# A two-model transformer kernel on one core: tiny attention placed between the blocks of the keys' projection, up and output projections as three products of rounded halves, and constant products in three of TensorE's waits

## What is computed

```python
h = modulate(rms_norm(x, norm_mix_g), sh_mix, sc_mix)
p_in = h @ w_in + b_in          # u, v, tq, tk, tv, nq, nk, nv, gates
tiny = tiny_attention(tq, tk, tv, tk_c, tv_c) @ tiny_w_o      # width 64, 256 queries, 512 keys
o_a = spatial_gating(u, v, tiny, ...)                         # 256 x 1024
o_b = neighbourhood_attention(nq, nk, nv, ...)                # 256 x 512
merged = gate_a * (o_a @ w_up_a) + gate_b * (o_b @ w_up_b)    # 1024x1024, 512x1024
x = x + g_mix * (merged @ w_out)                              # 1024x1024
h2 = modulate(rms_norm(x, norm_ffn_g), sh_ffn, sc_ffn)
y = moe_ffn(h2, ...)            # router, shared expert, 64 experts of width 256
```

## Time and profile before

| | us |
|---|---|
| median of three runs | 1713.54 (1712.35 to 1714.54) |
| the profiled execution, its own time | 1710.19 |
| its span, first to last instruction | 1708.3 |
| TensorE busy in it | 1632.5 (96%) |
| mean granted TensorE clock | 0.984 |

### The profile page before, as it was taken

The page is one execution under the profiler, slowest core; times in us unless marked ns, Lnnn a source line. Parts: engine busy times, 40 slices in busy tenths (PEclk is TensorE's granted clock), DMA queues, the critical chain, the costliest instruction groups (busy, mean ns, idle before and its releaser), DMA issues.

```text
span 1708.3 us, 21333 instructions
## 1 busy us (share of the span) xinstructions
PE 1632.5 (96%) x8924; PEld 1118.9 (65%) x8925; DVE 791.3 (46%) x1157; ACT 563.0 (33%) x796; POOL 40.9 (2%) x49
## 2 busy tenths in 40 slices
PE   5999999989999999999997999999999999999998
PEld 2745544447444444445454877799998877799997
DVE  3117934133222222222225685765445685776454
ACT  2013430012111111111113575644433566734341
POOL 0410010000000000000000000000000000000000
PEclk9998999998999999999998999999999999999999
DMA  9944873642999999999993433556546444546450
GB/s 357 283 145 142 307 288 117 251 169 105 390 420 421 421 421 421 420 422 421 421 408 137 170 139 136 197 166 205 168 154 221 149 148 148 197 148 217 155 172 25
DMA packets 148287, 418.52 MB, mean 245 GB/s; under 512 B 6960, under 2 KB 55104, under 8 KB 123168
## 3 DMA queue, kind: packets, MB, share of 16 engines
q1 hardware_dynamic: 134688, 335.15, 53.0%
q10 hardware_dynamic: 8784, 63.97, 9.0%
q0 software_dynamic: 4720, 18.03, 3.5%
HBM read 416.07 MB, written 2.95 MB: 245 GB/s over the span
## 4 chain that ended last, share of the span: by engine, by line
PE 89%; DVE 5%; ACT 2%; issue 1%; SPq 1%; DMA 1%; DVEq 0%; ACTq 0%
PE bank L1303 14%; PE bank L1198 13%; PE bank L1517 12%; PE bank L897 10%; PE bank L1209 7%; PE bank L1467 6%; PE bank L1180 4%; PE bank L1219 3%; PE bank L866 3%; PE bank L1036 3%; PE bank L1488 3%; PE bank L1316 3%; PE bank L910 2%; SPq L704 1%; DVE ring_low L2266 1%
## 5 line engine op out<-in xcount | busy, mean ns | idle before, releaser
L2266 DVE TENSOR_TENSOR ring_low<-weight_ring,high_ring 128x2048 fp32r<-128x2048 f32 x92 | 207.9, 2288 | 58.4 <-ACT high_ring L1669 58.0
L1198 PE MATMUL bank<-weight_ring,arena 128*64 128x512 f32 x800 | 232.4, 593 | 1.7 <-issue 1.0
L1303 PE MATMUL bank<-high_ring,split 128*128 128x512 f32 x608 | 199.7, 402 | 0.8 <-DVE split L2273 0.8
L1669 ACT ACTIVATE high_ring<-weight_ring 128x2048 fp32r<-128x2048 f32 x92 | 171.6, 1905 | 10.5 <-PE bank L1303 5.9
L1198 PEld LDWEIGHTS bank<-weight_ring,arena 128*64 128x64 f32 x800 | 75.4, 137 | 149.1 <-issue 148.9
L897 PE MATMUL bank<-weight_ring,arena 128*128 128x512 f32 (+1 forms) x416 | 165.8, 560 | 3.9 <-ACT arena L1556 3.1
L1517 PE MATMUL bank<-split,ring_low 128*128 128x256 f32 x576 | 162.6, 282 | 0.0
L1303 PE MATMUL bank<-ring_low,split 128*128 128x512 f32 x384 | 154.3, 402 | 0.0
L1517 PE MATMUL bank<-split,high_ring 128*128 128x256 f32 x832 | 148.9, 280 | 0.0
L1303 PEld LDWEIGHTS bank<-high_ring,split 128*128 128x128 f32 x608 | 116.4, 192 | 32.5 <-issue 3.4
L897 PEld LDWEIGHTS bank<-weight_ring,arena 128*128 128x128 f32 x416 | 79.5, 196 | 86.7 <-issue 82.6
(11 more groups left out here) (295 smaller groups left out, 2440.5 us busy)
## 6 DMA issues: line engine op xcount, KB each, us to landing
weight_ring<-in_w_in SPq DMA_DIRECT2D x62, 1024.0 KB, 7.6
weight_ring<-in_w_e_gate SPq DMA_DIRECT2D x49, 1024.0 KB, 9.3
weight_ring<-in_w_e_up SPq DMA_DIRECT2D x49, 1024.0 KB, 12.8
weight_ring<-in_w_e_down ACTq DMA_DIRECT2D x46, 1024.0 KB, 10.0
weight_ring<-in_w_ada SPq DMA_DIRECT2D x24, 1024.0 KB, 13.6
weight_ring<-in_w_ffn_gate SPq DMA_DIRECT2D x22, 1024.0 KB, 5.5
weight_ring<-in_w_ffn_up SPq DMA_DIRECT2D x22, 1024.0 KB, 8.0
weight_ring<-in_w_ffn_down SPq DMA_DIRECT2D x22, 1024.0 KB, 5.3
```

The lines of the kernel that those rows point to most:

```text
L1198: last = mm(hidden_bank[side * CAP:(side + 1) * CAP, :].rearrange("p (j n) -> p j n", n=FF), xgT[:, p // 2 % 2, kt, at:at + CAP], hidden_u ...
L1303: last = mm(bank(key)[:, :], left[:, a_, n, t * P:(t + 1) * P], wv[b_][:, j, :], start=(n == 0 and i == 0), stop=(n == kts * len(units_) - ...
L1669: A(upper(key, layer), ring[:, units.place[key][0], :], ACT.Copy).then_inc(sem("high_ready"), 1)
L2266: V.tensor_tensor(lower(key), ring[:, units.place[key][0], :], upper(key, layer), ALU.subtract)\
```

## The change

On TensorE and with it on the engines that feed it:

- The four steps of the tiny attention (`tiny_turns`, `tiny_scores`, `tiny_probs_turn`, `tiny_sum`) each follow one of the four `nk` blocks; the same steps on ScalarE and VectorE stand between their work on those blocks, and `nv` comes last. `pr` and `prT` lie elsewhere.
- The weights of `upa`, `upb` and `wo` (10 pieces of 128x2048, `FIRST_SPLIT`), the gated rows, `obT` and the merged rows are split into halves; `token_split` takes the place of `token_major`. The gating and the up projections are reordered: the turns of tile 0 stand ahead of the last gating product, and `upa` and `upb` go by column half first, then by tile.
- `keep_busy(key, n)` issues n float32 products of constants into a free bank: 3 ahead of the `tiny` projections, 4 ahead of the turns of `h2`, 7 ahead of the second model's first turns, and 1 more in each of its two layers ahead of `vs`. Their results are not used.
- Loads: only the first of the shared expert's three is issued ahead of the last piece of `wo`; the other two follow the first six expert pieces and wait for the last two `wo` groups. The router's weights are loaded at the end of the gated rows' turns, the final norm's row later.

```diff
+FIRST_SPLIT = [("upa", 0, 0), ("upa", 0, 1), ("upb", 0), ("upa", 1, 0), ("upa", 1, 1), ("upb", 1),
+               ("wo", 0, 0), ("wo", 0, 1), ("wo", 1, 0), ("wo", 1, 1)]
+FIRST_UPPER = [20480, 24576, 10240, 22528, 12288, 24576, 20480, 10240, 22528, 12288]
...
-        oaT, mT = area(6144, KT, S), area(8192, KT, S)
+        oas = split[:, 6144:10240].rearrange("p (w k t) -> p w k t", w=2, k=KT)
+        obs = routed[:, 5888:7936].rearrange("p (w f t) -> p w f t", w=2, f=4)
         xn, cn = area(10240, TT, D), area(12288, TT, D)
...
+                        else:
+                            wait_full(sp, ("wo", 0, 1))
                     elif j == 0:
...
+            for j in (1, 2):
+                wait_full(sp, ("wo", j - 1, 1))
+                load_shared(j)
...
 
             wait_out(pool, ("oaT", 3))
-            pool.dma_start(fin_g, bcast("final_norm_g", 0, D)).then_inc(sem("fin_landed"), 16)
-            wait_full(pool, ("upb", 1, 1))
             pool.dma_start(w_rt, a["w_router"].rearrange("(k p) n -> p k n", p=P)).then_inc(sem("router_landed"), 16)
             pool.dma_start(rt_b, bcast("b_router", 0, E)).then_inc(sem("router_landed"), 16)
+            wait_full(pool, ("upb", 1, 1))
+            pool.dma_start(fin_g, bcast("final_norm_g", 0, D)).then_inc(sem("fin_landed"), 16)
...
+            def token_split(key, left, t, units_, kts, it, between=None):
+                wait_bank(pe, key, it)
+                n = 0
+                for uk in units_:
+                    if n and between:
+                        between()
+                    wait_split(pe, uk, it)
+                    wv = halves(uk, CHUNK, it)
+                    for j in range(kts):
+                        for i, (a_, b_) in enumerate(PASSES):
+                            last = mm(bank(key)[:, :], left[:, a_, n, t * P:(t + 1) * P], wv[b_][:, j, :],
+                                      start=(n == 0 and i == 0), stop=(n == kts * len(units_) - 1 and i == 2))
+                        n += 1
+                full(last, key)
...
+            def keep_busy(key, n, it=0):
+                wait_bank(pe, key, it)
+                for _ in range(n):
+                    mm(bank(key)[:, :], k("ident"), const[:, 0:CHUNK], start=True, stop=True)
...
+            keep_busy(("tiny", 0), 3)
...
-            for f in range(4):
+            def tiny_turns():
+                pe.wait_ge(sem("tiny_roped"), 1)
+                turns(("tqT", 0), [tqkv[:, t, 0:TINY] for t in range(TT)])
+                turns(("tkT", 0), [tqkv[:, t, TINY:2 * TINY] for t in range(4)])
+            def tiny_scores():
+                wait_out(pe, ("tqT", 0))
...
+            def tiny_probs_turn():
+                for t in range(TT):
...
+            def tiny_sum():
+                for t in range(TT):
+                    wait_out(pe, ("tpT", t))
+                    wait_bank(pe, ("tO", t))
...
+            for f, tiny_step in enumerate((tiny_turns, tiny_scores, tiny_probs_turn, tiny_sum)):
                 feature_major(("nk", f), hT.rearrange("p w k t -> p k w t"), 2 * S, both(("win", "nk")), (f,))
+                tiny_step()
...
+            gating(0, 0)
+            gating(0, 1)
+            gating(1, 0)
+            gated_turn(0)
+            gating(1, 1)
+            wait_tile(("oaT",), 0)
+            token_split(("upa", 0, 0), oas, 0, both(("upa", 0)), 4, 0)
+            gated_turn(1)
+            pe.wait_ge(sem("ob_low"), 1)
+            token_split(("upb", 0, 0), obs, 0, [("upb", 0)], 4, 0)
+            wait_tile(("oaT",), 1)
+            token_split(("upa", 0, 1), oas, 1, both(("upa", 0)), 4, 0)
+            token_split(("upb", 0, 1), obs, 1, [("upb", 0)], 4, 0)
+            token_split(("upa", 1, 0), oas, 0, both(("upa", 1)), 4, 0)
+            token_split(("upb", 1, 0), obs, 0, [("upb", 1)], 4, 0)
+            token_split(("upa", 1, 1), oas, 1, both(("upa", 1)), 4, 0)
+            pe.wait_ge(sem("merged"), 3)
             turn_tile(("mT",), mg, 0)
+            token_split(("upb", 1, 1), obs, 1, [("upb", 1)], 4, 0)
             wait_tile(("mT",), 0)
-            token_major(("wo", 0, 0), mT, 0, both(("wo", 0)), 4)
-            pe.wait_ge(sem("merged"), 2 * TT)
+            token_split(("wo", 0, 0), oas, 0, both(("wo", 0)), 4, 0)
+            pe.wait_ge(sem("merged"), 4)
             turn_tile(("mT",), mg, 1)
-            token_major(("wo", 1, 0), mT, 0, both(("wo", 1)), 4)
+            token_split(("wo", 1, 0), oas, 0, both(("wo", 1)), 4, 0)
             wait_tile(("mT",), 1)
             for n in range(2):
-                token_major(("wo", n, 1), mT, 1, both(("wo", n)), 4)
+                token_split(("wo", n, 1), oas, 1, both(("wo", n)), 4, 0)
+            keep_busy(("h2T", 0), 4)
             for t in range(TT):
...
+                if layer == 0:
+                    keep_busy(("l_xT", 0), 7)
                 input_turn(0)
+                keep_busy(("vs", 0), 1, layer)
                 wait_out(pe, ("l_xT", 0), layer)
...
+            def first_high(*key):
+                wait_weights(act, key)
+                A(upper(key, 0), ring[:, units.place[key][0], :], ACT.Copy).then_inc(sem("first_high_ready"), 1)
+            def first_turned(name, t):
+                for half in range(2):
+                    wait_full(act, (name, 2 * t + half))
+                    A(oas[:, 0, 4 * half:4 * half + 4, t * P:(t + 1) * P],
+                      bank((name, 2 * t + half))[:, :].rearrange("p (a b) -> p a b", b=P), ACT.Copy)\
+                        .then_inc(sem("first_turned"), 1)
...
+                    first_high("upa", 0, 0)
...
+            first_high("upa", 0, 1)
+            wait_full(act, ("row", 7))
+            wait_out(act, ("nrm", 1))
+            A(obs[:, 0], obT, ACT.Copy).then_inc(sem("ob_high"), 1)
+            first_turned("oaT", 0)
+            wait_full(act, ("sg", 1, 1))
+            first_high("upb", 0)
+            first_high("upa", 1, 0)
+            first_turned("oaT", 1)
+            first_high("upa", 1, 1)
...
+            first_high("upb", 1)
+            first_high("wo", 0, 0)
+            wait_full(act, ("upb", 0, 1))
+            first_high("wo", 0, 1)
+            first_turned("mT", 0)
+            wait_full(act, ("upa", 1, 1))
+            first_high("wo", 1, 0)
+            first_high("wo", 1, 1)
+            first_turned("mT", 1)
...
+            keys_low(0)
             dve.wait_ge(sem("nq_high"), 1)
             V.tensor_tensor(nqs[:, 1], nq32, nqs[:, 0], ALU.subtract).then_inc(sem("nq_low"), 1)
-            for t in range(4):
-                biased_out(("nv", t), nv[:, t, :])
+            keys_low(1)
...
+            def first_low(*key):
+                dve.wait_ge(sem("first_high_ready"), FIRST_SPLIT.index(key) + 1)
+                V.tensor_tensor(lower(key), ring[:, units.place[key][0], :], upper(key, 0), ALU.subtract)\
+                    .then_inc(sem("first_split_ready"), 1)
...
+            first_low("upa", 0, 1)
+            gated_out(1, 0)
+            first_turned_low("oaT", 0)
+            gated_out(1, 1)
+            dve.wait_ge(sem("ob_high"), 1)
+            V.tensor_tensor(obs[:, 1], obT, obs[:, 0], ALU.subtract).then_inc(sem("ob_low"), 1)
+            first_low("upb", 0)
...
+            branch_a(0, 0)
+            first_turned_low("oaT", 1)
+            first_low("upa", 1, 0)
+            branch_b(0, 0)
+            first_low("upa", 1, 1)
+            branch_a(0, 1)
+            branch_b(0, 1)
+            first_low("upb", 1)
+            branch_a(1, 0)
+            first_low("wo", 0, 0)
+            branch_b(1, 0)
+            first_low("wo", 0, 1)
+            branch_a(1, 1)
+            first_turned_low("mT", 0)
+            branch_b(1, 1)
+            first_low("wo", 1, 0)
+            first_low("wo", 1, 1)
+            first_turned_low("mT", 1)
```

More of the change, by code:

```diff
@@ L206, in plan @@
         main.take(("ts", t))
-    for t in range(TT):
-        main.take(("tpT", t))
-        main.take(("tO", t))
+    for name in ("tpT", "tO"):
+        for t in range(TT):
+            main.take((name, t))
     for i, (name, col) in enumerate((("v", COL_V), ("u", COL_U))):
@@ L1575, in _ @@
                 out(A(prT[:, t, :], bank(("tpT", t))[:, :], ACT.Copy), ("tpT", t))
+            keys_high(3)
+            for t in range(TT):
                 wait_full(act, ("tO", t))
```

191 lines of the change are left out of this document (98 added, 93 removed).

## The result

The changed kernel takes **1689.07 us** (median of 4 runs, 1685.15 to 1691.31) against 1714.04 us for the kernel before (4 runs, 1712.35 to 1718.43). The ratio is 0.9849 with a 95% interval of 0.9831 to 0.9867: 25 us faster, where 28.2 were forecast. A second set of runs on another chip gave 1689.62 against 1714.24.

The account below looks back on a forecast made before the run. TensorE, 89% of the chain, was taken to bound the kernel. The terms 2.8 + 6.7 + 13.7 + 5.0 + 0 = 28.2 us, off a runs' median of 1713.5, gave 1685.3 us; range 1680 to 1696.

Parts of the forecast that it names:

- term 1: Tiny projections behind the wait for `hT`: constant products keep the clock full there, saving 2.8 us.
- term 2: Tiny attention: its steps between the `nk` blocks hide TensorE's waits, saving 6.7 us.
- The fall at 39 came in the wait that is filled now: At `hT`: the clock fell in the wait the constants fill, the reason for taking 2.8 between -0.5 and 2.85.
- every chain is hidden with some 2 us to spare: Tiny attention: the longest partner chain, 3.3 us plus one `nk` copy, fits under a 6.9 us `nk` block.
- Term 3: Up and output projections: 240 one-pass instructions replace 160 of 0.429 us, and waits around the turns go, saving 13.7 us.
- gap of 216 ns: Split products in up and output projections run at the skill page's gap: 4.0 us under forecast, 1681.3, chance 0.04.
- The walk: Piece-by-piece check of the up and output projections: every half ready before its products, closest 347.3 for 347.7.
- late half: Rival in the up projection: halves late by 1 us at each of ten pieces, 10 us lost, 1695, chance 0.09.
- Term 4: Router and shared expert: constants in the wait for `h2` keep the clock full, saving 5.0 us.
- Term 5: Second model's start: seven products leave 3.0 us of a 9.00 us wait empty; gain 0, ends -0.2 and 1.0.
- one of them lost: Constants fail to hold the clock at `hT` or at router: 1688.5 to 1690.5; both lost 1693.6; rival's chance 0.16.
- the serial case: Up and output projections: copy, subtraction and products in series, 4.2 us a piece, 42 for ten: 1727.3, chance 0.02.

Follow-up runs that it names:

- the first profile: The profiled execution of the changed kernel, unedited, from its first set of runs: 1691.31 us, against 1710.19 us for the profiled kernel before.
- the best version: Changed kernel plus three constant products in each second-model layer, in the wait ahead of the fourth weighted sum: 1683.72 us, ratio 0.9823.
- The doubled copies: Changed kernel with ScalarE making each upper half of the ten up and output projection pieces twice: 1689.20 us, ratio 0.9853.
- the early group: Three more constant products ahead of those at `hT`, around the fourth modulation chunk: added to the changed kernel 1685.38 us; with the fourth weighted sum's wait filled too, 1685.98.

## Why the prediction came out right, and what in it was wrong

The time lay in the range and 3.8 us above the forecast. By the values measured below the terms add up to 24.6 us (0 + 5.2 + 13.4 + 5.0 + 1.0) for the 25 measured, so no large errors cancel. The two large terms came out by the mechanism that was forecast; what is missing is term 1 and a part of term 2. By its own terms:

**Term 1, 2.8 us: wrong.** It measured 0, give or take some 3 us (the kernel without that group is as fast). Two steps failed. "The fall at 39 came in the wait that is filled now": in five of seven profiles the clock falls between 34.9 and 37.4 already, behind the waits for weights, and then the constants run for 4.1 to 5.3 us in place of 2.7 and delay what they were to help. The tiny blocks ended at 51.3 to 55.7 in seven profiles with the group (mean 53.5), at 53.3 to 54.2 in five without (mean 53.7). Up to 33 to 35 us one execution that fell and one that didn't are alike to a tenth of a microsecond (0.07 and 0.08 busy from 33, the same wait of 1.59): nothing in these rows of the kernel's work decides it. By the Trainium skill, TensorE: Matmul & The Clock Gate, section Part 1: The HAM clock gate, the clock's measuring runs on whatever the kernel does; these two traces agree with it, though they don't show it. The other step is the silent one, that earlier tiny blocks make an earlier `nv`: where the clock held, they ended at 51.3, and TensorE then waited 1.27 and 3.49 us for the probabilities.

**Term 2, 6.7 us: 5.2 measured (2.6 to 6.0 by the interval).** The step "every chain is hidden with some 2 us to spare" costed VectorE's scaling at 0.49 from a row where GpSimd was idle. Moved 40 us ahead, it stands beside GpSimd's sum of 13.2 us and takes 5.4 to 9.1. Where that just fits, as in the first profile, the term was over by 0.6 for the steps and `nv` (the steps 5.7 us for 5.3, `nv` 27.68 for 27.47) and 0.4 for the wait behind `nv` (1.30 for 0.9). The stretch up to L1924 stayed VectorE's, as said: 9.9 us from the first scores to the read-out in both kernels.

**Term 3, 13.7 us: right.** 13.4 alone. From gating to the end of `wo` the best version takes 73.3 us for 87.2, 13.9. In the first profile it was 12.4, since the clock fell at 301 and 24 instructions took 6.88 us instead of 5.59. The 0.2325 an instruction was 0.233. The Trainium skill's gap of 216 ns didn't show in these products; the row was the better guide. The walk found no late half and there was none; its closest slack of 0.4 us was too small: the last piece was ready at 344.5 for 347.8.

**Term 4, 5.0 us: right.** Router and shared expert took 0.5 less in the turns and 4.5 less behind them. Without the group the same stage was, in all four later profiles, worse than in the profile of before (31.2 to 31.7 for 30.6), so its worth in a usual execution is 5.3 us rather than 4.5.

**Term 5, 0: about 1 us better,** by the stage, with the times undecided.

**The rivals.** The constants held the clock in one wait and not in the other, which is the rival's "one of them lost". Its price with the group at `hT` lost, 28.2 - 2.8 - 0.5 = 24.9 or 1688.6 us, is nearer to the 1689.07 than the forecast is. No half was late. The experts' pairs stayed at 14.86 us and their stage moved as a whole. The doubled copies refute the serial case. One cause of the missing 3.8 us stood in none of them: an engine off the chain, GpSimd, became the bound of an earlier start.

Not tried: a version in which the scaling of the probabilities stands behind GpSimd's sum (each tiny step one block later, or the sum cut in two). By the waits seen it could free up to 2 or 3 us where the tiny blocks end early.

## What to carry to other kernels

When work is moved ahead in time, look at what every other engine does at the new place, GpSimd too, and don't take its duration from the old place. A wait ahead of dense work is worth filling with products when the clock is still up at its start and little of the wait stays empty. At `h2`, with 1.0 us left empty, it worked every time (26.07 us in nine profiles of nine). At the second model's start the seven products ran at full clock, but 3.0 us stayed empty, and the turns behind them took 1.65 to 1.97 us in seven profiles of nine, 1.09 in two. A group behind other thin stretches, as at `hT`, gains and loses by turns. Compare stages over several executions before a difference of 3 us between two profiles is given to the change.

## What the hardware showed that was not expected

- One VectorE instruction of 0.49 us took 9.06, another of 1.23 took 14.07, each ending 0.3 or 1.1 us behind GpSimd's 13.2 us instruction; the second began 0.17 us behind GpSimd's, and took 1.23 where it began 0.6 us ahead.
- The kernel before varies by 3 us in 34 of 38 later executions and by 5.3 in all of them, the changed kernel by 9.3 in eight, from 1685.15 to 1694.49. With the wait of the fourth weighted sum filled the spread is 2.1 us in five executions, and 2.9 in five with the early group too. In the profiles the clock's falls come at different places; that they make the scatter is likely and not shown.
- The mean granted clock alone doesn't give the time: two executions of the kernel with the constants alone, both at 0.992, took 1701.27 and 1705.25 us. It counts where the clock is low.
